# Moving norm sums, tap products, chunk order and score order in a two-layer block plus a second attention block on one core

## What is computed

```python
# first block, layer 0: sliding-window attention and multi-scale pooling
# first block, layer 1 (odd mixer)
a, b, gate = split(h @ w_in)                 # 3 x 1024
glu  = a * sigmoid(b)
conv = depthwise_conv(glu, 31 taps)
y    = silu(layer_norm(conv)) * silu(gate)
x    = x + rms_norm(y @ w_out)
# second block, on 16 meta tokens + 1024 tokens
q, k, v, f, b_gate, c_gate, u = split(rms_norm(h) @ w_in)
y_attn = softmax(q k / 8 + cum_i - cum_j, causal) v     # 8 heads of 64
y_conv = b_gate * conv3(c_gate * u)
h = h + concat(head_norm(y_attn), head_norm(y_conv)) @ w_out
h = h + square(relu(rms_norm(h) @ w_ff1)) @ w_ff2
```

## Time and profile before

| | us |
|---|---|
| three timed runs | 2036.91, 2032.13, 2035.73 |
| their median | 2035.73 |
| the profiled execution, its own time | 2034.13 |
| the span of its profile | 2032.3 |
| PE busy | 1947.0 (96%) |
| DVE, POOL, ACT busy | 1300.5, 1139.9, 725.4 |
| mean granted clock of TensorE | 0.985 of full speed |

### The profile page before, as it was taken

How to read it: one execution, slowest core, us unless ns; L and a number is a source line. 1 busy time by engine, 2 the same in 40 slices (tenths; PEclk the granted TensorE clock), 3 DMA queues, 4 the chain that set the end, 5 groups by cost and what they waited for, 6 DMA issues and landing times.

```text
span 2032.3 us, 24978 instructions
## 1 busy us (share of the span) xinstructions
PE 1947.0 (96%) x9212; PEld 1563.5 (77%) x9212; DVE 1300.5 (64%) x1852; ACT 725.4 (36%) x1209; POOL 1139.9 (56%) x936
## 2 busy tenths in 40 slices
PE   7999999999999999899999899999999999999997
PEld 6887877887777788778887565687788887888885
DVE  6127563679997996351673477467544447777778
ACT  3002653442245542330210455324322324545542
POOL 3221115569988995435542100127877878988885
PEclk9999999999999999999999899999999999999999
DMA  5431117455544554438523543335657668676652
GB/s 192 144 120 69 42 42 254 170 182 182 178 168 156 172 181 146 165 133 247 179 85 94 125 86 74 134 136 175 214 195 233 219 206 311 217 257 210 216 189 101
DMA packets 104504, 335.43 MB, mean 165 GB/s; under 512 B 12672, under 2 KB 12928, under 8 KB 103616
## 3 DMA queue, kind: packets, MB, share of 16 engines
q1 hardware_dynamic: 55616, 192.74, 29.4%
q0 software_dynamic: 30384, 106.44, 15.4%
q10 hardware_dynamic: 18384, 34.66, 4.6%
HBM read 272.75 MB, written 46.20 MB: 157 GB/s over the span
## 4 chain that ended last, share of the span: by engine, by line
PE 42%; issue 31%; POOL 21%; DVE 4%; DMA 1%; ACT 1%; POOLq 0%; ACTq 0%; DVEq 0%
PE PS L1215 28%; PE PS L1760 12%; POOL WL L983 12%; POOL RBM L1022 3%; POOL SQH L1022 2%; POOL WH L976 2%; DMA WH<-weights 1%; DVE ACC L3274 1%; DVE ACC L3295 1%; DVE OT L3349 0%; PE PS L1669 0%; DVE PS L2662 0%; DVE PS L2682 0%; POOL G L1024 0%; DVE OPL L3250 0%
## 5 line engine op out<-in xcount | busy, mean ns | idle before, releaser
L1215 PE MATMUL PS<-XHM,WH 128*128 128x512 f32 (+2 forms) x1464 | 524.1, 382 | 24.7 <-POOL WL L983 11.6
L1215 PE MATMUL PS<-XLM,WH 128*128 128x512 f32 (+2 forms) x1464 | 511.0, 373 | 0.0
L1215 PE MATMUL PS<-XHM,WL 128*128 128x512 f32 (+2 forms) x1464 | 510.9, 373 | 0.0
L976 POOL DMA_DIRECT2D WH<-weights x149 | 85.6, 574 | 704.5 <-PE PS L1215 687.6
L983 POOL TENSOR_TENSOR WL<-WRAW,WH 128x1024 fp32r<-128x1024 f32 x149 | 362.2, 2431 | 34.3 <-DMA WH<-weights 22.0
L1215 PEld LDWEIGHTS PS<-XHM,WH 128*128 128x128 f32 x1464 | 271.3, 190 | 86.5 <-POOL WL L983 17.9
L1215 PEld LDWEIGHTS PS<-XLM,WH 128*128 128x128 f32 x1464 | 277.8, 190 | 49.8 <-issue 1.7
L1215 PEld LDWEIGHTS PS<-XHM,WL 128*128 128x128 f32 x1464 | 277.2, 189 | 48.8
L2713 DVE SCALAR_TENSOR_TENSOR PS<-G,TAPW,PS 128x512 f32<-128x512 f32 x319 | 215.8, 753 | 0.6
L3274 DVE TENSOR_TENSOR ACC<-ACC,PS 128x1024 f32<-128x1024 f32 (+1 forms) x113 | 119.8, 1073 | 15.8 <-PE PS L1215 12.9
L1215 PE MATMUL PS<-OPH,VSH 128*128 128x512 f32 x256 | 99.9, 390 | 2.8 <-issue 2.5
(11 more groups left out here) (381 smaller groups left out, 3973.8 us busy)
## 6 DMA issues: line engine op xcount, KB each, us to landing
WRAW<-weights SPq DMA_DIRECT2D x211, 512.0 KB, 3.5
WH<-weights POOLq DMA_DIRECT2D x195, 512.0 KB, 4.5
OPR<-inner SPq DMA_DIRECT2D x56, 512.0 KB, 6.6
inner<-STAGE ACTq DMA_DIRECT2D x56, 256.0 KB, 4.3
inner<-TOUT ACTq DMA_DIRECT2D x48, 256.0 KB, 4.5
XTOK<-x SPq DMA_DIRECT2D x8, 512.0 KB, 7.7
x_kept<-X SPq DMA_DIRECT2D x4, 1024.0 KB, 7.1
X<-x_kept SPq DMA_DIRECT2D x8, 512.0 KB, 5.0
```

The lines of the kernel that those rows point to most:

```text
L976: g.dma_start(WH[:, u, :], weights[WORDER[p]]).then_inc(w_hi[u], 16)
L1215: m = nc.tensor.matmul(dst[:, a:b], w, v[:, a:b], start=first and n == 0, stop=last and n == 2)
```

## The change

1. First half of the layer norm: PE's `half_sum(0, H_LN)` and `half_wide(0, H_LN)` move from the end of job `P_IN1C+2` and the middle of `P_IN1C+3` to k = 1 and k = 6 of `P_IN1C+2`. ACT's `half_root` moves ahead of the last sigmoid, and the tap products are spread anew (places 3, 5 and 7 of `gated_hi` instead of 1, 3 and 6). DVE's `half_inverse` comes two taps after `mids` instead of five.
2. Second half: `half_sum` moves two k-steps and `half_wide` three k-steps ahead. `two_jobs` (the first two jobs of `P_OUT1B` in turns, k by k) becomes two ordinary half jobs.
3. The `H_POST1` and `H_MIX` sums of the second half move into the key jobs, and one of the scaled banks of (1, `H_MIX`) is 4 instead of 6, which takes away a DVE wait.
4. The chunks `P_REST+7` and `P_REST+8` are done in turns: 4 k-steps, 2 of the other, 4, 6. The new semaphore `rows_left` is raised after the second k-step of `P_REST+8`. Slot 0's POOL preparation, ACT's copy `slot_queries(0)` and SP's `slots(0)` wait for `rows_left` instead of the end of the chunk. On SP `slots(0)` stands ahead of the load of `P_OUT2+1`, and `slots(1)`, `max_rows(1)` ahead of `P_OUT2+2`.
5. `scores` run two units ahead of `values` instead of one, except at the end of a pair of heads. Roots, reciprocals and the splits of the heads' output come one unit later.
6. `out2` starts with one k-slice of its first tile, then the last `head_norm`, and the last k-slices of the first two tiles are put in another order.

```diff
@@ PE: layer 1
-                    hooks = {2: ((7, lambda: half_sum(0, H_LN)),), 3: ((5, lambda: half_wide(0, H_LN)),)}.get(i, ())
+                    hooks = {2: ((1, lambda: half_sum(0, H_LN)), (6, lambda: half_wide(0, H_LN)))}.get(i, ())
...
-                    hooks = ((0, lambda: half_sum(1, H_LN)), (5, lambda: half_wide(1, H_LN))) if c == 2 else ()
+                    hooks = {1: ((6, lambda: half_sum(1, H_LN)),), 2: ((2, lambda: half_wide(1, H_LN)),)}.get(c, ())
...
-                two_jobs(P_OUT1B, (OUT1, 0, 1), (OUT1, 1, 1), X_OUT1[1])
-                for k in range(2, KD):
-                    half_job(P_OUT1B + k, (OUT1, k, 1))
+                for k in range(KD):
+                    half_job(P_OUT1B + k, (OUT1, k, 1), X_OUT1[1] if k == 0 else None)
@@ PE: last chunks, attention, out2
-            chunk(P_REST + 7, X_IN2[1], hooks={k: (tile(0, k),) for k in range(KD)})
...
+            chunk(P_REST + 7, X_IN2[1], hooks=tiles0, ks=range(4))
+            chunk(P_REST + 8, X_IN2[1], rows_done=1, ks=range(2))
+            chunk(P_REST + 7, X_IN2[1], hooks=tiles0, ks=range(4, KD))
...
                 scores(0)
+                scores(1)
+                max_turn(1)
...
-                    if n + 1 < NU:
-                        scores(n + 1)
+                    ahead = n + (1 if (n + 2) % (2 * PER_HEAD) == 0 else 2)
+                    while begun <= min(ahead, NU - 1):
+                        scores(begun)
+                        begun += 1
...
+            out2(0, ORDER2[:1])
+            head_norm(2 * HEADS - 1)
+            out2(0, ORDER2[1:-1])
+            out2(1, ORDER2[:-2])
+            out2(0, ORDER2[-1:])
+            out2(1, ORDER2[-2:])
@@ ACT
-            tap_products(P_IN1C)
             sigmoid_b(1, 6)
+            half_root(0, H_LN)
             tap_products(P_IN1C + 1)
             sigmoid_b(1, 7)
-            half_root(0, H_LN)
-            tap_products(P_IN1C + 2)
-            gated_hi(0, ((1, lambda: tap_products(P_IN1C + 3)), (3, lambda: tap_products(P_IN1C + 4)),
-                         (6, lambda: tap_products(P_IN1C + 5))))
+            gated_hi(0, ((3, lambda: tap_products(P_IN1C + 2)), (5, lambda: tap_products(P_IN1C + 3)),
+                         (7, lambda: tap_products(P_IN1C + 4))))
...
-                if s == 5 and c >= 1:
+                if s == 6 and c >= 1:
                     roots(c - 1)
@@ SP
+            slots(0)
             load(P_OUT2 + 1)
             max_rows(0)
+            slots(1)
+            max_rows(1)
             load(P_OUT2 + 2)
```

More of the change, by code:

```diff
@@ L474, in build @@
         m2_neg = sem("m2_neg")
+        rows_left = sem("rows_left")
         m2_turned = sem("m2_turned")
@@ L752, in slots @@
                     sp.wait_ge(s2_full, PER_HEAD * (h - 1))
+                elif h == 0:
+                    sp.wait_ge(rows_left, 1)
                 else:
@@ L799, in _ @@
             load(P_OUT2)
+            slots(0)
             load(P_OUT2 + 1)
             max_rows(0)
+            slots(1)
+            max_rows(1)
             load(P_OUT2 + 2)
-            for c in range(PAIRS):
+            extended(1)
+            for c in range(1, PAIRS):
                 slots(2 * c)
-                if c >= 1:
-                    max_rows(2 * c)
+                max_rows(2 * c)
                 slots(2 * c + 1)
@@ L1103, in _ @@
                     initialized(1)
+                if p == P_OUT2:
+                    pool.wait_ge(rows_left, 1)
+                    init_slot(0)
+                    initialized(2)
                 if p == P_OUT2 + 1:
                     pool.wait_ge(psum_full, USE[C_OUT2])
-                    init_slot(0)
-                    initialized(2)
                     init_slot(1)
@@ L1217, in three, with chunk @@
                 return m
-            def chunk(p, x_ready, meta=False, hooks=None):
+            def chunk(p, x_ready, meta=False, hooks=None, rows_done=None, ks=range(KD)):
                 c = WORDER[p]
                 u, use = p % NW, USE[c]
-                pe.wait_ge(w_ready, p + 1)
                 first = p < P_OUT0[0]
-                pe.wait_ge(evacuated, max(use - 2, USE0) if first else use - 1)
-                for k in range(KD):
+                if ks[0] == 0:
+                    pe.wait_ge(w_ready, p + 1)
+                    pe.wait_ge(evacuated, max(use - 2, USE0) if first else use - 1)
+                for k in ks:
                     for hook in (hooks or {}).get(k, ()):
@@ L1256, in half_job @@
                 m.then_inc(half_full, 1)
[L1258 to L1271, removed]
             def front_job(p, job, before, hooks=()):
@@ L1848, in _ @@
             chunk(P_REST + 6, X_IN2[1])
-            chunk(P_REST + 7, X_IN2[1], hooks={k: (tile(0, k),) for k in range(KD)})
-            chunk(P_REST + 8, X_IN2[1], hooks={1: (lambda: max_turn(0),), 3: (tile(1, 0),), 4: (tile(1, 1), tile(1, 2)),
-                                                5: (tile(1, 3),), 6: (tile(1, 4),), 7: (tile(1, 5),)})
+            tiles0 = {k: (tile(0, k),) for k in range(KD)}
+            chunk(P_REST + 7, X_IN2[1], hooks=tiles0, ks=range(4))
+            chunk(P_REST + 8, X_IN2[1], rows_done=1, ks=range(2))
+            chunk(P_REST + 7, X_IN2[1], hooks=tiles0, ks=range(4, KD))
+            chunk(P_REST + 8, X_IN2[1], hooks={3: (lambda: max_turn(0),), 4: (tile(1, 0), tile(1, 1)),
+                                                5: (tile(1, 2), tile(1, 3)), 6: (tile(1, 4),), 7: (tile(1, 5),)},
+                  ks=range(2, KD))
             max_tile(1, 6)
             max_tile(1, 7)
-            max_turn(1)
             attention2()
[L1856 to L1859, removed]
+            out2(0, ORDER2[:1])
[4 more added lines that the diff above has]
+            out2(1, ORDER2[-2:])
             for n in range(2, KD):
@@ L2843, in _ @@
             mids(0)
-            conv(1, 1, 3, 8)
+            conv(1, 1, 3, 5)
             half_inverse(0, H_LN)
-            conv(1, 1, 8, 10)
+            conv(1, 1, 5, 10)
             normed(0, ((2, lambda: glu(1, 5)), (5, lambda: glu(1, 6))))
@@ L3070, in _ @@
                 c, s = divmod(n, 2 * PER_HEAD)
[L3071 to L3073 removed]
+                if 7 <= s < 11 and c >= 1:
+                    inverse(c - 1, s - 7)
+                if s == 11 and c >= 1:
                     scaled(c - 1)
[L3075 removed]
+                if s == 13 and c >= 1:
                     heads_lo(c - 1)
```

27 lines of the change are left out of this document (13 added, 14 removed).

## The result

| | before | changed |
|---|---|---|
| median of five runs, us | 2032.13 | 2022.56 |
| lowest, highest | 2031.64, 2036.91 | 2017.41, 2024.35 |
| ratio, 95% interval | | 0.9938, 0.9925 to 0.9951 |
| profiled execution, its own time | 2034.13 | 2017.41 |
| span of its profile | 2032.3 | 2015.6 |

What follows compares the result with a forecast made beforehand. PE, busy for 96% of the span, was taken to bound the kernel. Six gains sum to 23.2 us, less 3.4 for the clock 19.8; from the median 2035.7 that gives 2015.9, forecast as 2015, range 2007 to 2025.

Steps and rivals of the forecast that it cites:

- E: Pairs of heads (1145 to 1290), scores two units ahead: gain of 0.7 us, bounds -1 and 2.5.
- signs of being wrong: Wrong if: ACT idle on POOL (silu slices), POOL on ACT's products, PE on ACT (first pair), exponential waits above 5 us.
- A: First layer norm (about 600 to 673): earlier root and silu, limited by POOL; gain of 6.0 us, bounds 3 and 7.5.
- Rival 2: First layer norm's gain given back as POOL's gap repeats at following positions: gain 13.8 us, time 2020; chance 0.12.
- Rival 4: Slower: late tap products hold POOL's weights and PE; at 2 us per sum the time is 2040; chance 0.06.
- B: Second layer norm (798 to 843): earlier low slices, jobs one after the other; gain of 6.4 us, bounds 4.7 and 8.
- C: Norms after the second layer norm (870 to 912): sums and spreading sooner; gain of 0.3 us, ends 0 and 2.4.
- D: Start of the attention (1087 to 1145): head 0's copies early, first scores fill a wait; 7.7 us, bounds 3.3 and 8.1.
- F: `out2` (1288 to 1316): one k-slice fills the wait, third weight sooner; gain of 2.1 us, bounds 0.7 and 3.6.
- Clock: Three new waits may each cost 1.7 us by the clock; two of three taken, 3.4 us off the gain.
- Rival 1: Every new wait costs the clock, 1.7 us each: gain 16.4 us, time 2018; chance 0.15.

## Why the prediction was right and where it failed

The time, 2022.6, lay inside the range and on the forecast side, but 7.6 us above the forecast. That is kinder than the gain: of the 19.8 us forecast, 9.6 came by the medians and 12.6 by the ratio, as the kernel before took 2032.13 at the median of five runs and not the 2035.73 counted from. At the edited places the traces have 11.2, and E alone is 7.9 of the 8.6 us that are missing. That the time is in the range is so in part luck, since a step of it failed that no rival named. Two of the signs of being wrong did show: POOL was idle once for a product of ACT, and the waits for exponentials came to 6.8 us, above 5. By the steps:

- **A, 6.0 forecast:** right in mechanism. POOL gave 5.3 of the 6.06 us, the new wait at `P_OUT1A+5` was 2.12 us (forecast 2 to 3), the clock took 1.6 behind it, and a wait of 0.6 for a norm's sum that came later before is gone: 4.5 is left. Rival 2 (given back at each position) did not come. Rival 4 came in small: the 0.8 that lack of 6.06 are POOL's 0.79 us of idle time at 625.49, for a tap product that stood ahead of the first silu in ACT's list and now stands behind the first slices. Behind that POOL filled 32.9 of the 33 us from 630 to 663.
- **B, 6.4:** 6.0, with the forecast waits for slices, and without the loss of clock that I allowed for.
- **C, 0.3:** the sign was wrong. The stage itself, from 870 to 912, lost 0.5 us, between the two traces as in the experiments with and without part 3. The table's 0.3 has 0.8 in it from near 955, where two waits for POOL's weights are gone. ACT's copies were named as what stands ahead of the high parts; that they move later with the longer key job was not seen.
- **D, 7.7:** 7.3, and 6.7 by itself. The copies were there, and the scores of units 0 and 1 took 2 of the 3.4 us of the wait for the maxima, as forecast.
- **E, 0.7:** this is the step that failed, at -7.2, outside its bounds of -1 and 2.5. I priced the later root and its table loads on ACT, and nothing of what moved with it on DVE: four reciprocals of 1.7 us, a scaling of 1.3 and a split of 1.2 per pair, all ahead of the maxima's reductions in the same queue. One unit later they stand ahead of larger reductions, and PE waits 0.8 and 1.4 us where it waited 0.4. ACT's later root by itself cost 1.2 us of idle time, the places of DVE's work and of the splits 4.3. What is queued behind a moved step was worked out for SP and not for DVE. The gain of the second unit ahead, the positive part of the term, was not there either.
- **F, 2.1:** 0.3. The later half (1.4 sooner for the third weight) came: 1.93 became 0.56. The earlier half failed on the bank: the slice that was to fill the wait writes the bank that DVE empties at the end of that wait, so 2.2 us of idle time became 1.7, and the half-clock stretch behind took 1.7 more. A slice of the other tile does fill it.
- **Clock, 3.4:** two of the new waits cost a half-clock stretch (663, 1274) and the 1.43 ahead of `max_turn` a third; B's did not. Rival 1 looks nearer by this than I took it, but only the stretch at 663 came in every kernel that has its wait; the other two came in some, as the last section shows.

## What to carry to other kernels

A piece of work that is moved by one place in one engine's list takes its whole queue along: price what comes behind it on each engine that it touches, above all where the neighbours grow from place to place. A filler for a wait must not need what ends the wait; check the bank that it writes as well as what it reads. Where two queues are at parity with PE, relieving one shows the other: here 2.1 us of POOL turned into 2.4 us of DVE.

## What the runs showed of the hardware that was not expected

Equal waits don't cost equal clock. The 1.43 us ahead of `max_turn` stand in twelve of the kernels. In three of them, the changed one among them, the 4 us behind that wait ran at 0.57 of the clock, in the other nine at 1.00. Here are these 4 us in the changed kernel, then in the one with two units ahead and old places:

```profile
1104.07:1108.07 4.00, 4.00 (x14) 2.82 (x15) 0.28 (x1) 1.23 (x4) 3.68 (x5) 0.57 0.90 187
```

```profile
1107.14:1111.14 4.00, 4.00 (x21) 2.91 (x22) 0.28 (x1) 1.83 (x5) 3.68 (x5) 1.00 0.88 183
```

The 1.71 us at the start of `out2` were followed by 0.57 to 0.65 of the clock in three kernels and by 1.00 in four. The 2.1 us at the sixth output job were followed by 0.57 to 0.59 in all eleven kernels that have them. The ACT waits of 2.0 us at the roots were followed by a half-clock stretch in some kernels and not in others with the same waits: the stretch of the pairs ran at 0.97, 0.98, 0.99 or 1.00 of the clock, worth up to 3.5 us of busy time (137.9 against 134.4). Two kernels whose PE waits agree at the start of the attention and in the pairs differed by 4 us in the median (2012.98 against 2008.62, in two sets of runs on two chips), and five runs of the changed kernel lie between 2017.4 and 2024.4 with clocks of 0.990 to 0.987. Differences below that are read better from one place in two traces than from medians.
